# Hybrid retention and sliding-window attention block: reordered ScalarE and VectorE streams in attention, later slab loads at the start of retention

## The reference, cut to what matters

```python
scores = (jnp.einsum('bqhgd,bkhd->bhgqk', qn, keys).astype(jnp.float32)
          - slopes * dist.astype(jnp.float32))
scores = jnp.where(valid, scores, -jnp.inf)
m = jnp.maximum(jnp.max(scores, axis=-1, keepdims=True), sink)
p = jnp.exp(scores - m)
probs = p / (jnp.sum(p, axis=-1, keepdims=True) + jnp.exp(sink - m))
return jnp.einsum('bhgqk,bkhd->bqhgd', probs.astype(vals.dtype), vals)
```

## Time and profile before

| | |
|---|---|
| median of 3 runs | 1626.28 us (1625.79 to 1626.64) |
| the profiled execution, its whole time | 1628.11 us |
| its span in the profile | 1626.3 us |
| PE, DVE, ACT, POOL busy in the span | 99%, 65%, 48%, 25% |
| mean granted clock of TensorE | 0.997 |
| retention | about 329 to 485 us |
| attention | about 501 to 736 us |

### The profile page before, as it was taken

One profiled execution on the slowest core, in us unless ns is written; L12 is line 12 of the kernel. 1 busy time (PEld: TensorE's weight loads), 2 busy tenths in 40 slices (PEclk: granted clock), 3 DMA queues, 4 the chain that ended last, 5 costly groups with the idle time before them and its releaser, 6 DMA issues.

```text
span 1626.3 us, 22775 instructions
## 1 busy us (share of the span) xinstructions
PE 1603.7 (99%) x7942; PEld 1336.6 (82%) x7942; DVE 1062.0 (65%) x2063; ACT 783.0 (48%) x1615; POOL 405.2 (25%) x584
## 2 busy tenths in 40 slices
PE   9999999999999999999999999999999999999999
PEld 7888888878888787878888788888888888888887
DVE  7984556665566778767564438866666556766675
ACT  6733244554555777763222126655555544444442
POOL 0111011121125898884221000122111122100000
PEclk9999999999999999999999999999999999999999
DMA  8432323255444665668553222354444389733452
GB/s 298 177 109 111 118 95 106 102 197 185 161 154 117 163 182 152 178 165 246 176 188 123 71 65 108 117 190 150 148 149 143 121 307 360 247 97 98 147 182 92
DMA packets 132113, 255.95 MB, mean 157 GB/s; under 512 B 15024, under 2 KB 52320, under 8 KB 132000
## 3 DMA queue, kind: packets, MB, share of 16 engines
q1 hardware_dynamic: 88304, 135.89, 26.2%
q0 software_dynamic: 43408, 118.48, 22.1%
q10 hardware_dynamic: 288, 0.14, 0.0%
HBM read 159.67 MB, written 69.47 MB: 141 GB/s over the span
## 4 chain that ended last, share of the span: by engine, by line
PE 87%; DVE 4%; POOL 3%; DMA 2%; ACT 2%; issue 1%; ACTq 0%; DVEq 0%
PE bank L1226 28%; PE bank L1231 27%; PE bank L1230 27%; POOL PR L1102 2%; DMA PW<-PR 1%; ACT PR L2172 1%; POOL RT L1118 1%; DVE PTL L2957 1%; DVE PR L2949 1%; PE bank L1529 1%; DMA RAW<-in_w_in 1%; PE bank L1561 1%; PE bank L1543 1%; ACT PTH L2149 0%; PE bank L1269 0%
## 5 line engine op out<-in xcount | busy, mean ns | idle before, releaser
L1226 PE MATMUL bank<-WH,ADH 128*128 128x512 f32 x448 | 174.3, 389 | 0.0
L1230 PE MATMUL bank<-WH,ADL 128*128 128x512 f32 x448 | 174.3, 389 | 0.0
L1231 PE MATMUL bank<-WL,ADH 128*128 128x512 f32 x448 | 174.3, 389 | 0.0
L2340 ACT CAST ADH<-ARAW 128x512 fp32r<-128x512 f32 x112 | 69.5, 621 | 169.6 <-PE bank L1231 157.6
L1102 POOL TENSOR_SCALAR PR<-PR,RC 128x272 f32<-128x272 f32 (+1 forms) x128 | 140.1, 1260 | 39.7 <-DVE RC L2982 39.7
L3238 DVE TENSOR_TENSOR ADL<-ARAW,ADH 128x512 fp32r<-128x512 f32 x112 | 77.5, 692 | 97.0 <-ACT ADH L2340 96.9
L1226 PE MATMUL bank<-HN,WH 128*128 128x512 f32 x344 | 138.3, 402 | 0.0
L1231 PE MATMUL bank<-HN,WH 128*128 128x512 f32 x344 | 135.8, 395 | 0.0
L1230 PE MATMUL bank<-HN,WL 128*128 128x512 f32 x344 | 135.7, 394 | 0.0
L1226 PE MATMUL bank<-SOPH,WH 128*128 128x512 f32 x256 | 99.8, 390 | 0.0
L1231 PE MATMUL bank<-SOPL,WH 128*128 128x512 f32 x256 | 99.6, 389 | 0.0
(11 more groups left out here) (392 smaller groups left out, 4314.7 us busy)
## 6 DMA issues: line engine op xcount, KB each, us to landing
ARAW<-uop SPq DMA_DIRECT2D x112, 256.0 KB, 3.2
uop<-US POOLq DMA_DIRECT2D x64, 256.0 KB, 3.0
WRAW<-in_w_up SPq DMA_DIRECT2D x15, 1024.0 KB, 6.2
PW<-PR SPq DMA_DIRECT2D x56, 272.0 KB, 2.5
RAW<-in_w_in SPq DMA_DIRECT2D x52, 256.0 KB, 4.6
uop<-UA POOLq DMA_DIRECT2D x48, 256.0 KB, 3.2
proj<-SA POOLq DMA_DIRECT2D x36, 256.0 KB, 2.3
RT<-proj POOLq DMA_DIRECT2D x8, 1024.0 KB, 8.5
```

The lines of the kernel that those rows point to most:

```text
L1226: mm = pe.matmul(bank, ahi, bhi, start=first, stop=False, skip_group_check=onto)
L1230: pe.matmul(bank, alo, bhi, start=False, stop=False, skip_group_check=onto)
L1231: return pe.matmul(bank, ahi, blo, start=False, stop=last, skip_group_check=onto)
L2340: act.copy(ADH[:, n % 4, :], ARAW[:, n % 4, :]).then_inc(da_hi, 1)
```

## The change

It has two parts.

**At the turn into retention**, GpSimd issues `load_rt(0)`, the stores 4, 5 and 6, and then `load_rt(1)`; `load_rt(2)` and `load_rt(3)` move behind the first gate store of chunks 0 and 1. ScalarE and VectorE no longer split blocks 4 to 6 of slab 1 ahead of the loop: all four blocks 4 to 7 are split at n = 0, on ScalarE behind the `QS` copy, on VectorE behind `KD` and the two copies of `STA`.

**In attention**, on ScalarE `take_next_q` and `weigh(T)` move ahead of `take_y`, `hi_q`, `hi_kn`, `hi_v` and all splits (`take_p` stays ahead of them). On VectorE `top(T)` moves ahead of `lo_p(T-3)`, and `inverse(T)` comes right behind `lo_p`, ahead of everything else.

The streams of TensorE and SyncE stay as they are, and no computing instruction is added or removed.

```diff
@@ gpsimd
             load_rt(0)
             store_gx(4)
+            store_gx(5)
+            store_gx(6)
             load_rt(1)
-            store_gx(5)
-            for n in range(2, 4):
-                load_rt(n)
-            store_gx(6)
...
                 store_gate(ACT_B + 2 * n, n // 4, 2 * n % 8)
+                if n < 2:
+                    load_rt(n + 2)
@@ scalar (vector alike, with split_lo)
-            for k in range(4, KT - 1):
-                split_hi(SLAB_B, k)
...
                     if r == 0:
-                        for k in range(4 if it else KT - 1, KT):
+                        for k in range(4, KT):
                             split_hi(SLAB_B + it, k)
@@ scalar, attention
                 if LAG <= T < NPAIR + LAG:
                     take_p(T - LAG)
+                if T in NEXT_Q:
+                    take_next_q(*NEXT_Q[T])
+                if T < NPAIR:
+                    weigh(T)
                 if T >= LAG + 2 and T % 2 == 1:
...
-                splits = new_slabs(T) if T <= NPAIR + 1 else []
-                for slab, k in splits[:2]:
-                    split_hi(slab, k)
-                if T < NPAIR:
-                    weigh(T)
-                for slab, k in splits[2:]:
+                for slab, k in new_slabs(T) if T <= NPAIR + 1 else []:
                     split_hi(slab, k)
@@ vector, attention
                     take_next_k(*NEXT_K[T])
+                if T < NPAIR:
+                    top(T)
                 if LAG <= T < NPAIR + LAG:
                     lo_p(T - LAG)
-                if T < NPAIR:
-                    top(T)
...
+                if T < NPAIR:
+                    inverse(T)
                 if T % 8 == 0 and T // 8 + 1 < NB:
                     normed_q(T // 8 + 1)
-                    for slab, k in splits[:1]:
-                        split_lo(slab, k)
-                    inverse(T)
                     normed_kn(T // 8 + 1)
-                    splits = splits[1:]
...
-                for slab, k in splits[:1]:
-                    split_lo(slab, k)
-                if T < NPAIR and not (T % 8 == 0 and T // 8 + 1 < NB):
-                    inverse(T)
-                for slab, k in splits[1:]:
+                for slab, k in splits:
                     split_lo(slab, k)
```

More of the change, by code:

```diff
@@ L2193, in _ @@
                     hi_v(T // 8 + 1).then_inc(qh_rdy, 1)
-                if T in NEXT_Q:
-                    take_next_q(*NEXT_Q[T])
                 if T > NPAIR + 1:
@@ L2751, in _ @@
                 gx_swish(6, f)
-            for k in range(4, KT - 1):
-                split_lo(SLAB_B, k)
             def flatten_q():
```

## The result

The changed kernel took 1632.89 us in the median of 5 runs (1631.47 to 1635.73), the kernel before 1625.79 us in the median of 5 runs beside them (1625.18 to 1626.64). The ratio is 1.0048, with a 95% interval of 1.0037 to 1.0059: slower by 7.8 us (7.1 by the two medians), where 9.8 us less were forecast. The time lies outside the predicted range, on the side of the fourth rival.

What follows compares the result with a forecast made beforehand. TensorE was taken as the bound, busy 1603.7 of 1626.3 us, so only its waits could be won. Terms -6.2 - 3.4 + 0.4 - 0.6 = -9.8 us gave 1616.5 us, range 1610.5 to 1623.5.

Steps and rivals of the forecast that it cites:

- the fourth rival: Attention: `PTL` late at most of 28 `values`, up to 1.0 us each; slower needs 0.47 us each on average; chance 0.07.
- The turn, -6.2: Turn into retention: TensorE's 3.5 us wait for `QS` and 2.7 us of half clock go, saving 6.2 us.
- Six of seven waits for `PW`, -3.4: Attention: the earlier reciprocal removes six of TensorE's seven waits for `PW`, saving 3.4 us; bounds -5.8 and 0.
- the ping-pong: Attention before the change: `PTH` cast waits for exponentials, these for the maximum, which stands behind `PTL`, which waits for `PTH`.
- The delay of `lo_p`, the part of +0.4 that was worked out: Attention: `lo_p` behind `top` makes `PTL` just in time for `values`; +0.4 us in all, bounds -3 and +5.
- The first burst, 0 with bounds of -4 and +2: Attention steps 9 to 12, eight splits: the 2.43 us gap changes its name and keeps its size, 0 us.
- the second "the same, milder": Attention steps 37 to 40: same as steps 9 to 12, the gap keeping its size, but milder.
- The early reciprocal: Attention: the reciprocal comes 1 to 1.5 us earlier on average, shortening the pair's chain.
- The end of attention, -0.6: End of attention: no `top` is left, so the first of the late products gains its part, 0.6 us.
- The third: Rival, attention: GpSimd becomes the limit, waits for `PW` only move, 3.4 us stay, 1620 us; chance 0.11.

Runs made afterwards that it cites:

- turn alone: Kernel before with only the change at the turn into retention (loads `RT`, splits of slab 1): 1621.57 us, -4.6 us against the kernel before.
- swap_only: Turn alone plus one exchange on VectorE, the maximum ahead of `lo_p`; reciprocal, splits and ScalarE as before: -4.9 us against the kernel before.
- inv_split: swap_only with the reciprocal put forward to just behind `lo_p` and the step's first split, except where T mod 8 = 0: -2.9 us against the kernel before.
- dve_only: Turn alone plus VectorE's new order in attention, ScalarE's order as before: 1627.82 us, +1.8 us against the kernel before.
- hi_back: Changed kernel with only the casts `hi_q`, `hi_kn`, `hi_v` put back ahead of the exponentials on ScalarE: 0.0 us against the kernel before.
- attn_only: Kernel before with only the new order of ScalarE and VectorE in attention, old turn: 1636.58 us, +11.2 us against the kernel before.
- hi_splits_back: Changed kernel with both the casts `hi_q`, `hi_kn`, `hi_v` and the next slab's splits put back: -1.5 us against the kernel before.
- splits_back: Changed kernel with splits put back: first two ahead of the exponentials on ScalarE, first one ahead of the reciprocal on VectorE: 1629.41 us, +3.7 us against the kernel before.
- lo_first: Changed kernel with only `lo_p` put back ahead of the maximum on VectorE: 1659.03 us.

## Why the prediction was wrong, step by step

**What the second part costs, edit by edit.** Each step is a difference of two measured versions, and each has an uncertainty of some 2 us:

```
turn alone                                                        -4.6
maximum ahead of lo_p                      swap_only              -0.3
reciprocal forward, behind first split     inv_split              +2.0
all splits behind the reciprocal           dve_only               +4.7
exponentials ahead of take_y and splits    hi_back                -1.8
hi_q, hi_kn, hi_v behind the exponentials  changed kernel         +7.8
sum                                                               +7.8
```

The step of dve_only also moves `normed_q` behind the reciprocal in one step of eight. The price of a step holds in this sequence only: put on VectorE's old order, ScalarE's new one costs 31 us, and here its two steps cost 6.0. Forecast and result are 17.6 us apart: 7.8 of it are the casts, 4.7 the splits, 2.7 the waits for `PW` less the forecast delay of `lo_p`, 2.0 the reciprocal, 1.6 the turn; -1.2 is what remains.

*The turn, -6.2.* Right in its mechanism, its places and its landings (4.7 us, forecast 3 to 5), and in its size against the one trace that it was read from. The runs have it at 4.6, with 6.2 at the end of the interval: the gap of 3.5 us and the half clock behind it belong to that execution, and attn_only shows the same program with 1.57 us and the full clock. That the span of 1626.3 us equalled the median of 1626.28, by which the prediction took a saving in the span off the median, was chance too: that execution was 1.8 us above the median.

*Six of seven waits for `PW`, -3.4.* They went, and so did the ping-pong. But the gain did not reach the end: swap_only shows most clearly that what leaves line 1543 comes back at line 1561. The sum took a removed wait as time won although the next input, `PTL`, had 0.05 us to spare by the prediction's own count.

*The delay of `lo_p`, the part of +0.4 that was worked out.* The count was nearly right: `PTL` ends 2.06 us behind the scores (593.59 + 0.69 - 592.22), forecast 1.9, and TensorE is there at 1.95 (the rows are of hi_back). The net of this term and the one before it is small, -0.3 us.

**The step that failed** is the sentence behind it: "Behind VectorE's own waits are queued: `lo_q`, `lo_kn` and `lo_v` now wait for casts that ScalarE does only behind the exponentials (about 0.8 us a time, 3 times a block of 8 steps), and the splits wait alike." Number and size were right: 21 waits, 13.9 us, 0.66 each. They were priced at nothing: `values` got +0.4 in all, with a slack of 0.05 us just counted. The runs price the casts at 7.8 us. The bound of +5 for this term was too low as well. And the range held less than it claimed: the upper bounds of its own terms (-3.7 for the turn, 0 for `PW`, +2, +5, -0.6) add up to +2.7, that is 1629.0 and not 1623.5.

*The first burst, 0 with bounds of -4 and +2, and the second "the same, milder".* Measured in the sum of lost time: +2.6 and +4.2. The gap did change its name, from `PW` to `PTL`, but did not keep its size. The prediction counted how many splits stand ahead of `PTL`, and not that the change makes VectorE wait ahead of the first of them, for the exponentials and then for `WH` (1.3 us in the rows at 524.52). The splits' place is worth 4.1 to 4.7 us.

*The early reciprocal* was counted only as a gain of the chain. It is also a wait of VectorE, which in the old place the other work ahead of it fills in part (10.6 us of waits in swap_only, 19.8 in inv_split). The prediction priced no such wait; it costs about 2 us here with `lo_p` as a filler, and 17.4 without it in a version that has the splits behind it as well.

*The end of attention, -0.6.* From the scores of pair 63 to the first product behind attention it is 16.0 us instead of 13.8. TensorE waits there for the last `PW`:

```profile
737.64 0.60 PE L1543 MATMUL bank<-IDR,PW 128*128 128x128 f32 x4 [2.78 <-DMA PW<-PR]
```

```profile
DMA to landing us min/median/max: 5.8/5.8/5.8
```

The second row is the landing of the copy into `PW` issued at 731.8: it took 5.8 us, where the last five of the kernel before took 2.4 in the median. The kernel with part 2 alone, with the same order there, waits 0.3 us for `PW`, and its last copy took 3.3 us. hi_splits_back has it again, 5.3 us and a wait of 2.3, hi_back and splits_back have 3.3 and 3.2. So this 2.8 us and the half clock behind it look like chance, whose own time is among the longer two of five (1635.58; the others are 1631.47, 1631.88, 1632.89 and 1635.73). I have not shown it.

**The rivals.** The fourth had the right symptom, `PTL` late at `values`, but the size falls short: by the sum of lost time line 1561 loses 18.8 us in attention instead of 5.9, and at the 26 `values` of blocks 1 to 7 that come before the last scores 0.59 us each instead of 0.20, so 0.39 us more where 0.47 was asked. Its reason was half of the truth: it rested on the place of `lo_p`, and swap_only clears that. The third is refuted: GpSimd's multiplications got longer, but until the last pair no wait for `PW` is left. In attention, changed kernel and then before:

```profile
L1102 POOL TENSOR_SCALAR PR<-PR,RC 128x272 f32<-128x272 f32 (+1 forms) x127 | 157.1, 1475 | 33.0 <-DVE RC L2975 33.0
```

```profile
L1102 POOL TENSOR_SCALAR PR<-PR,RC 128x272 f32<-128x272 f32 (+1 forms) x128 | 140.1, 1260 | 39.7 <-DVE RC L2982 39.7
```

The mean rises from 1260 to 1475 ns, 17 us in all, where 12 us had been estimated. It all fits into idle time. This is the contention that the Trainium skill states (SBUF — State Buffer, Who interferes with whom). By that rule, the trace agrees: in the changed kernel 50 of the 112 multiplications of 272 columns have a VectorE instruction with two SBUF inputs beside them and take 1825 ns in the mean, the other 62 take 1363; before, it was 30 with 1424 and 82 with 1300. Here it cost nothing that shows.

What stays open is how much of the 2.0 us of the early reciprocal is real, and how the old turn's price is spread over executions, since only two traces show it.

## What to carry to other kernels

When an order is changed on two engines that hand work to each other, list every wait that it makes on the engine that feeds the bottleneck, and price each at its full length unless slack is shown: 21 waits of 0.66 us ahead of an input with 0.05 us of slack cost 7.8 us, though a third of them turned out to be free. Work that "is not urgent" may be what fills the time in which an urgent instruction would block its engine; moved behind it, the engine waits first and does the work afterwards. And a wait that goes is only worth the slack of the next input: see what that is before it is counted as won.

## What the runs showed that I had not expected

A mismatch of the two orders can cost much more than either order, and in one direction only: with ScalarE's new order the time is 1652.6 us on VectorE's old one and 1632.9 on its new one, and both new orders with `lo_p` alone put back give 1659.0; VectorE's new order on ScalarE's old one takes 1627.8. All these kernels issue the same instructions, and the busy time of TensorE in the slowest of them, 1614.0 us in lo_first, is within 11 us of the others. The page shows where time is spent, and hardly that 33 us are lost.
